# A two-layer trunk with attention and experts: feature-major second attention, a reordered opening, and a router fed by unnormalised rows

## The chip, the cores and the metric

The kernel runs on one core of one Trainium2 chip. The metric is the device time of one execution in microseconds (us), as the median of several runs. The engines are TensorE (PE in the profile), VectorE (DVE), ScalarE (ACT), GpSimd (POOL) and SyncE (SP, which issues most of the transfers).

## What is computed

Two layers over 256 positions of width 1024, one sequence. All of it is float32; the large products are made of three products of a high and a low part (`w_hi`, `w_lo`). For the parts that the change touches the reference says:

```python
mod = (cond @ ada_w[layer] + ada_b[layer])[:, None, :]
sh_m, sc_m, g_m, sh_f, sc_f, g_f = jnp.split(mod, 6, axis=-1)
h = _rmsnorm(x, gn[0]) * (1.0 + sc_m) + sh_m          # ahead of each of the four sub-layers
x = x + g_m * _rmsnorm(y, gn[1])                      # behind it

# second layer's attention (8 heads; 128 plain + 64 rotated features each)
c_q, c_kv, k_rope = jnp.split(h @ w_in, [256, 384], axis=-1)
q = (_rmsnorm(c_q, g_q) @ w_q_up).reshape(B, S, 8, 192)
kv = (_rmsnorm(c_kv, g_kv) @ w_kv_up).reshape(B, S, 8, 256)
# rotate q_rope and k_rope by position, causal softmax of q.k * 192**-0.5, times v, @ w_out

# second layer's experts
logits = (h @ w_router) + b_router                    # top 2 of 8, softmax of the two
```

The first layer has a stick-breaking attention and a dense gated product of width 2816.

## The kernel before

**Stages.** In order of time: the opening (sum of `ada_w` over the 8 parts of the condition vector, first normalisation), the first attention (to about 157 us), the dense product (to 359), the second attention (to 479), the router (to 504), eight or more visits to experts of some 47 us each, and the combination.

**Weights.** SyncE brings pieces of up to 128x2048 (1 MB) into a ring of six in one fixed order, `stream`; it issues piece n when piece n-6 is freed (`freed`). For a weight piece, ScalarE makes the high part (`hi`, L515) once the product before last is done (`used`), VectorE the low part (`lo`, L837), which frees the slot, and TensorE then multiplies. For a piece of `ada_w`, VectorE alone adds it to `acc` scaled by one column of the condition (L850, L853). Each engine has its own handwritten order and the semaphores tie them.

**Modulation.** `mod_columns` (L1380) is 16 products of one column each on TensorE that sum `acc` over the partitions into shift and scale columns; `mod_cols` on VectorE adds the bias. `transpose_xhat` (L1371) turns the normalised rows into feature-major form. `modulated` (L883, L876) applies scale and shift on VectorE, 128x256 at a time, in four blocks of two; ScalarE casts each block (L557), VectorE makes its low part, and the products wait for it (`hTlo`). `keep_clock` (L1413) are filler products. There are three such boundaries with `modulated`: v=0 in the opening, v=1 ahead of the dense product, v=2 ahead of the second attention. v=3 feeds the router and the experts.

**Second attention.** The products with `mla_in` are token-major, 448 columns wide. ScalarE squares and sums the latents, VectorE scales them (`lat`), TensorE turns them (L1551), VectorE applies the gain (`cT`). q and kv are made token-major; ScalarE copies them out (L682, L688), VectorE rotates (L1082 and on), TensorE turns them back (L1579 to L1597), and four large copies follow. Then scores (L1606, L1607), a mask added by VectorE (L1112), two maxima, exponentials on ScalarE from SBUF, division, turning (L1614), a copy back (L1131), products with the values (L1479) and the output product with four weight pieces.

**Router.** `residual`, then ScalarE sums the squares of the new `x`, VectorE normalises into `xhat`, TensorE turns it (L1652), and 16 products with the router's weights give the logits (L1662). VectorE finds the top two and each row's place (L1175 and on); selection products (L1683) gather the first expert's rows.

## Time and profile before

| | |
|---|---|
| median of 3 runs | 901.51 us (900.4 to 906.21) |
| the profiled execution | 900.82 us |
| its span, first to last instruction | 899.3 us |
| mean granted TensorE clock | 0.972 of full speed |
| TensorE matmul busy | 837.3 us (93%) |
| VectorE busy | 705.9 us (78%) |
| ScalarE busy | 524.3 us (58%) |
| chain that ended last | PE 81%, DVE 12%, ACT 2%, DMA 2% |
| from HBM | 257.82 MB |

The busy share of TensorE is high nearly everywhere, and matmuls are pipelined, so it doesn't say whether the engine does useful work at full speed. The stages at the layer boundaries and the second attention have to be read by themselves, in windows and in order of time. The granted clock has two levels, 1.0 (2.4 GHz) and 0.5 (1.2 GHz); a mean between them is a mix in time. A float32 product shows as two records.

### The profile page before, as it was taken

The page shows a single profiled execution, that of the slowest core. Times are in us where ns is not written, and L with a number is a line of the kernel's source. Part 1 is how long each engine was busy: PE and PEld are TensorE (multiplying, and loading weights), DVE is VectorE, ACT ScalarE, POOL GpSimd, SP SyncE. Part 2 cuts the span into 40 slices and gives each one's busy share as a digit, 9 for nine tenths or more (in the row PEclk, how much of TensorE's full clock was granted, in tenths as well). Part 3 has the DMA queues.
Part 4 walks back from the last instruction along what each step waited for, and adds up shares of the span by engine and source line. Part 5 has one row for each costly group of instructions (what it writes and reads, how often), then busy time and mean ns, then how long its engine had stood idle before and what let it go on. Part 6 is the DMA issues. An engine that isn't in the chain of part 4 may idle for free.

```text
span 899.3 us, 12482 instructions
## 1 busy us (share of the span) xinstructions
PE 837.3 (93%) x4720; PEld 741.3 (82%) x4720; DVE 705.9 (78%) x585; ACT 524.3 (58%) x531; POOL 37.9 (4%) x46
## 2 busy tenths in 40 slices
PE   2999999899999999988798899999999999999993
PEld 2999777899999888877677788888888888888882
DVE  4888677876666988553855988898988889898977
ACT  2224924444444434334545678787979787878873
POOL 1001001000000101010000300000000000000120
PEclk9899999899999999689999999999999999999998
DMA  9989867297778998379912799999999999999991
GB/s 341 410 306 377 302 253 286 97 353 262 268 271 300 368 344 322 117 264 420 390 47 61 254 396 343 422 359 419 360 408 360 408 365 406 385 386 393 368 373 47
DMA packets 46239, 283.52 MB, mean 315 GB/s; under 512 B 5855, under 2 KB 5858, under 8 KB 19834
## 3 DMA queue, kind: packets, MB, share of 16 engines
q1 hardware_dynamic: 41002, 268.80, 77.7%
q0 software_dynamic: 3312, 12.06, 3.3%
q10 hardware_dynamic: 1888, 2.15, 0.7%
q8 instruction: 26, 0.43, 0.2%
q14 instruction: 11, 0.09, 0.0%
HBM read 257.82 MB, written 25.17 MB: 315 GB/s over the span
## 4 chain that ended last, share of the span: by engine, by line
PE 81%; DVE 12%; ACT 2%; DMA 2%; issue 2%; ACTq 1%; DVEq 0%; SPq 0%
PE ps L1712 9%; PE ps L1713 9%; PE ps L1717 9%; PE ps L1358 6%; PE ps L1360 6%; PE ps L1361 6%; PE ps L1320 5%; PE ps L1322 5%; PE ps L1321 5%; PE ps L1735 4%; PE ps L1729 4%; PE ps L1730 4%; DVE acc L853 3%; DVE w_lo L837 2%; PE ps L1380 2%; DMA ring<-in_moe_w_down 2%
## 5 line engine op out<-in xcount | busy, mean ns | idle before, releaser
L1169 DVE TENSOR_TENSOR w_lo<-ring,w_hi 128x2048 fp32r<-128x2048 f32 (+1 forms) x96 | 209.7, 2202 | 38.1 <-ACT w_hi L733 36.8
L515 ACT ACTIVATE w_hi<-ring 128x2048 fp32r<-128x2048 f32 (+2 forms) x58 | 109.7, 1893 | 198.0 <-PE ps L1361 100.6
L837 DVE TENSOR_TENSOR w_lo<-ring,w_hi 128x2048 fp32r<-128x2048 f32 (+2 forms) x58 | 138.3, 2385 | 77.1 <-ACT w_hi L515 77.1
L733 ACT ACTIVATE w_hi<-ring 128x2048 fp32r<-128x2048 f32 (+1 forms) x96 | 175.7, 1839 | 20.4 <-PE ps L1717 11.9
L1358 PE MATMUL ps<-hT_lo,w_hi 128*128 128x256 f32 x480 | 137.8, 287 | 4.6 <-DVE hT_lo L876 2.4
L1360 PE MATMUL ps<-hT_hi,w_hi 128*128 128x256 f32 x480 | 136.7, 285 | 0.0
L1361 PE MATMUL ps<-hT_hi,w_lo 128*128 128x256 f32 x480 | 136.7, 285 | 0.0
L853 DVE SCALAR_TENSOR_TENSOR acc<-ring,cond,acc 128x2048 f32<-128x2048 f32 x42 | 98.7, 2349 | 2.7
L1712 PE MATMUL ps<-w_hi,xe_hi 128*128 128x512 f32 (+1 forms) x256 | 97.7, 382 | 2.5 <-DVE xe_lo L1243 2.5
L1358 PEld LDWEIGHTS ps<-hT_lo,w_hi 128*128 128x128 f32 x480 | 93.2, 194 | 5.7 <-issue 2.8
L1169 DVE TENSOR_TENSOR m_lo<-ring,m_hi 128x2048 fp32r<-128x2048 f32 (+2 forms) x48 | 92.7, 1932 | 6.3 <-ACT m_hi L733 6.3
L1713 PE MATMUL ps<-w_hi,xe_lo 128*128 128x512 f32 (+1 forms) x256 | 96.3, 376 | 0.0
L1360 PEld LDWEIGHTS ps<-hT_hi,w_hi 128*128 128x128 f32 x480 | 93.2, 194 | 0.0
L1361 PEld LDWEIGHTS ps<-hT_hi,w_lo 128*128 128x128 f32 x480 | 93.1, 194 | 0.0
L733 ACT ACTIVATE m_hi<-ring 128x2048 fp32r<-128x2048 f32 (+2 forms) x48 | 78.0, 1625 | 8.9 <-PE ps L1717 6.4
L1717 PE MATMUL ps<-w_lo,xe_hi 128*128 128x512 f32 (+1 forms) x256 | 65.1, 376 | 0.0
L1712 PEld LDWEIGHTS ps<-w_hi,xe_hi 128*128 128x128 f32 x256 | 48.1, 188 | 9.9 <-issue 2.6
L1713 PEld LDWEIGHTS ps<-w_hi,xe_lo 128*128 128x128 f32 x256 | 48.1, 188 | 7.3
L1717 PEld LDWEIGHTS ps<-w_lo,xe_hi 128*128 128x128 f32 x256 | 47.4, 188 | 7.7
L1729 PE MATMUL ps<-w_hi,eT_hi 128*128 128x512 f32 x128 | 50.7, 396 | 0.0
L1730 PE MATMUL ps<-w_hi,eT_lo 128*128 128x512 f32 x128 | 50.0, 391 | 0.0
L1320 PE MATMUL ps<-w_lo,hT_hi 128*128 128x512 f32 (+1 forms) x112 | 45.4, 405 | 3.7 <-DVE hT_lo L876 2.1
(289 smaller groups left out, 1442.2 us busy)
## 6 DMA issues: line engine op xcount, KB each, us to landing
ring<-in_moe_w_gu SPq DMA_DIRECT2D x64, 1024.0 KB, 7.1
ring<-in_ada_w SPq DMA_DIRECT2D x48, 1024.0 KB, 6.9
ring<-in_moe_w_down SPq DMA_DIRECT2D x40, 1024.0 KB, 8.3
ring<-in_moe_w_gu SPq DMA_DIRECT2D x32, 768.0 KB, 8.9
ring<-in_ffn_w_gu SPq DMA_DIRECT2D x22, 1024.0 KB, 5.0
ring<-in_sb_w_in SPq DMA_DIRECT2D x12, 1024.0 KB, 7.5
ring<-in_ffn_w_down SPq DMA_DIRECT2D x11, 1024.0 KB, 6.1
x_rows<-blank SPq DMA_DIRECT2D x1, 8704.0 KB, 27.1
```

What stands on the lines that cost most here:

```text
L515: act.activation(w_hi[m % 2][:, 0:cols_n], ring[n % R][:, 0:cols_n], ACT.Copy).then_inc(hi_done, 1)
L733: act.activation(m_hi[k % NB][:, 0:n_c], ring[(N0 + k) % R][:, 0:n_c], ACT.Copy).then_inc(hi_done, 1)
L837: dve.tensor_tensor(w_lo[m % 2][:, 0:cols_n], ring[n % R][:, 0:cols_n], w_hi[m % 2][:, 0:cols_n].bitcast(F32), ALU.subtract).then_inc(free ...
L853: dve.scalar_tensor_tensor(dst, ring[n % R][:, :], cond[:, k:k + 1], dst, ALU.mult, ALU.add).then_inc(freed, 1)
L1169: dve.tensor_tensor(m_lo[k % NB][:, 0:n_c], ring[(N0 + k) % R][:, 0:n_c], m_hi[k % NB][:, 0:n_c].bitcast(F32), ALU.subtract).then_inc(free ...
L1320: pe.matmul(out, a_hi, b_lo, start=start, stop=False)
L1358: pe.matmul(o, w_h, hT_lo[:, k0 + k, :], start=(begin and k == 0 and f % 2 == 0), stop=False, skip_group_check=True)
L1360: pe.matmul(o, w_h, hT_hi[:, k0 + k, :], start=False, stop=False, skip_group_check=True)
L1361: ins = pe.matmul(o, w_l, hT_hi[:, k0 + k, :], start=False, stop=(end and k == 3 and f % 2 == 1), skip_group_check=True)
L1712: pe.matmul(o, xe_hi[:, 2 * q + h, :], bh[:, h, s, :], start=q + h == 0, stop=False)
L1713: pe.matmul(o, xe_lo[:, 2 * q + h, :], bh[:, h, s, :], start=False, stop=False)
L1717: ins = pe.matmul(ps[:, 2 * j + s, 0:gw[j]], xe_hi[:, 2 * q + h, :], bl[:, h, s, :], start=False, stop=q == 3 and h == 1)
```

## The change

1. **Opening.** ScalarE issues only the transfers of `x`, the latent gains, the frequencies and the positions ahead of its first work; those of the router and the gate biases go behind the first normalisation, whose scaling it now does itself. VectorE adds the eighth piece of `ada_w` in two halves, and TensorE sums the shift half while the scale half is added. `hi(1)` goes behind `modulated_hi(0)`.
2. **Modulation.** Of the four blocks, VectorE makes 0 and 3, ScalarE 1 and 2. Of `mod_columns(3)` only the shift half stays ahead of the second attention, the scale half goes to the router stage. Fillers ahead of the second attention are 5+5 instead of 8+8.
3. **Second attention.** All is feature-major: `mla_in` (padded to 512 columns, the rotated key twice) and both up-projections are computed transposed. The q latents aren't normalised; the root of their squares (`qs`, by token) is the scale of the exponential. The kv latents are scaled by a reciprocal of 128x256. Rotation is a product with a sign-and-swap matrix (`turn_half`) and with tables `trigT`. The causal mask is one float32r product per head (`later_r`). Exponentials are read from PSUM. Two of the four copies of turned probabilities go to ScalarE.
4. **Router.** TensorE turns `x` itself; logits are multiplied by the reciprocal root of the row where the bias is added. `xhat` is made by ScalarE behind the first expert piece's `hi`.

The core of the diff (long runs of the old second attention, declarations and host layout are left out):

```diff
 # ScalarE
+            for c in range(TC):
+                act.wait_ge(rstd_done, c + 1)
+                act.activation(xhat[:, c, :], x[:, c, :], ACT.Copy, scale=rstd[:, 0, c:c + 1]).then_inc(xhat_done, 1)
             act.dma_start(wr[:, :, :], w_router[0].rearrange("(k p) n -> p k n", p=P)).then_inc(s_small, 16)
             act.dma_start(br[:, :], b_router).then_inc(s_small, 16)
...
             hi(0)
+            modulated_hi(0)
             hi(1)
-            modulated_hi(0)
...
+                modulate(1)
+                for b in range(4):
+                    if b == 2:
+                        modulate(2)
+                    if b in (0, 3):
+                        act.wait_ge(t_done, 2 * v + b // 3 + 1)
+                    else:
+                        act.wait_ge(t_act, 2 * v + b)
...
             hi(M + 2)
+            act.wait_ge(cT_ok, 1)
+            act.activation(cT_hi[:, 0:2, :], cT[:, 0:2, :], ACT.Copy).then_inc(cThi, 1)
+            act.activation(sq[:, 0:2, :].rearrange("p k t -> p (k t)"), ps[:, 0, :], ACT.Square).then_inc(sq_ok, 1)
+            act.wait_ge(used, M + 2)
+            act.activation(sq[:, 2, :], ps[:, 1, 0:T], ACT.Square).then_inc(sq_ok, 1)
+            act.activation(kra[:, :], ps[:, 1, T:2 * T], ACT.Copy).then_inc(kra_ok, 1)
             hi(M + 3)
...
+            act.wait_ge(sum_mm, 1)
+            act.activation(root_kv[:, :], ps[:, 0, 0:T], ACT.Sqrt, scale=1.0 / KVL, bias=eps[:, 0:1]).then_inc(root_kv_ok, 1)
+            act.activation(qs[:, :], ps[:, 0, T:T + TC], ACT.Sqrt, scale=float(QW) / QL, bias=eps[:, 1:2]).then_inc(qs_ok, 1)
+            act.wait_ge(cT_ok, 2)
+            act.activation(cT_hi[:, 2, :], cT[:, 2, :], ACT.Copy).then_inc(cThi, 1)
             hi(M + 4)
...
             ehi(0, 0)
+            x_turned(1)
+            squares(6, 1, x[:, 1, :], mjunk)
+            root(6, 1)
+            for c in range(TC):
+                act.wait_ge(rstd_done, TC * 6 + c + 1)
+                act.activation(xhat[:, c, :], x[:, c, :], ACT.Copy, scale=rstd[:, 6, c:c + 1]).then_inc(xhat_done, 1)
             ehi(0, 1)
 # VectorE
-            ada(2)
-            normalise(0)
-            ada(DC - 2)
+            ada(3)
+            for c in range(TC):
+                inverse_root(0, c)
+            ada(DC - 4)
...
+            for a, done in ((0, ada_half), (1, freed)):
+                half = slice(a * D, (a + 1) * D)
+                dve.scalar_tensor_tensor(acc[:, half], ring[n % R][:, half], cond[:, n:n + 1], acc[:, half], ALU.mult,
+                                         ALU.add).then_inc(done, 1)
             lo(0)
...
             lo(M + 2)
+            dve.wait_ge(lat_q, 1)
+            for k in range(2):
+                ins = dve.tensor_scalar(cT[:, k, :], ps[:, 0, k * T:(k + 1) * T], lat_g[:, k:k + 1], None, ALU.mult)
             ins.then_inc(cT_ok, 1)
...
             lo(M + 3)
+            dve.wait_ge(kt_ok, 1)
+            dve.wait_ge(root_kv_ok, 1)
+            link(dve.reciprocal(root_kv[:, :], root_kv[:, :]))
+            dve.tensor_tensor(cT[:, 2, :], kt[:, :], root_kv[:, :], ALU.mult).then_inc(cT_ok, 1)
+            dve.wait_ge(qs_ok, 1)
+            dve.reciprocal(qs[:, :], qs[:, :]).then_inc(qs_ok, 1)
+            dve.wait_ge(qra_ok, 1)
+            cos, sin = (trigT[:, n, :].unsqueeze(1).broadcast_to([P, 4, T]) for n in range(2))
+            dve.tensor_tensor(qrT[:, :, :], qra[:, :, :], cos, ALU.mult).then_inc(qr_ok, 1)
+            dve.wait_ge(cThi, 2)
+            dve.tensor_tensor(cT_lo[:, 2, :], cT[:, 2, :], cT_hi[:, 2, :].bitcast(F32), ALU.subtract).then_inc(cTlo, 1)
+            lo(M + 4)
+            dve.wait_ge(kr_mm, 1)
+            dve.wait_ge(cT_ok, 2)
+            link(dve.tensor_tensor(kt[:, :], ps[:, 1, 0:T], trigT[:, 1, :], ALU.mult))
...
+            link(dve.tensor_tensor(qt[:, :, :], ps[:, 2:4, :].rearrange("p b (a t) -> p (b a) t", a=2), sin, ALU.mult))
+            dve.tensor_tensor(qrT[:, :, :], qrT[:, :, :], qt[:, :, :], ALU.add).then_inc(qr_ok, 1)
...
             row_max(0)
+            lo(M + 1)
             row_max(1)
...
+            residual(2, 5, [ps[:, 0:2, :], ps[:, 2:4, :]], 0)
+            mod_scale(3, 7)
...
             x_turned(0)
             x_turned(1)
+            dve.tensor_copy(lg_add[:, :], ps[:, 7, 0:E]).then_inc(bias_ok, 1)
 # TensorE
+            mod_columns(2, 0, (0,))
+            pe.wait_ge(trig_ok, 1)
...
+            mod_columns(2, 0, (1,))
+            keep_clock(5, 2)
+            mod_columns(3, 0, (0,), 2 * DC)
+            keep_clock(5, 2)
             transpose_xhat(2, 4)
+            gate_spread(2, 2)
...
+                product_T(M + h, 4 * h, 0, h == 0, h == 1, v=2, half_way=lat_q if h == 1 else None)
...
+            q_up(0)
+            pe.wait_ge(sq_ok, 2)
+            pe.wait_ge(kt_ok, 1)
...
+            pe.matmul(ps[:, 1, 0:T], turn_half[:, :], kra[:, :], start=True, stop=True).then_inc(kr_mm, 1)
+            q_up(1)
...
+                if h == 0:
+                    pe.wait_ge(kr_ok, 2)
+                if h == 2:
+                    pe.wait_ge(qs_ok, 1)
+                if h == 4:
+                    pe.wait_ge(qr_ok, 2)
...
+            turn_rows(0)
+            mod_columns(3, 7, (1,))
+            keep_clock(2, 6)
+            turn_rows(1)
```

## Rows read from the trace of the kernel before

**Rows 1.** Two windows: start:end, us, busy us (instructions), clock, DMA share, GB/s
```profile
12.00:33.00 21.00, 15.22 (x109) 14.65 (x110) 19.99 (x15) 6.19 (x11) 0.00 (x0) 1.00 1.03 413
358.90:380.10 21.20, 19.13 (x113) 18.89 (x112) 10.52 (x20) 7.14 (x12) 0.00 (x0) 0.68 0.33 124
```

**Rows 2.** Timeline of the opening: start us, us, engine line op, [idle before <-releaser]
```profile
10.63 1.28 ACT L551 ACT_TABLE_LOAD   x1 [10.63 <-issue]
17.98 14.62 DVE L853 SCALAR_TENSOR_TENSOR acc<-ring,cond,acc 128x2048 f32<-128x2048 f32 x6
30.70 1.91 ACT L515 ACTIVATE w_hi<-ring 128x2048 fp32r<-128x2048 f32 x1 [14.36 <-DMA ring<-in_sb_w_in]
32.65 2.29 DVE L837 TENSOR_TENSOR w_lo<-ring,w_hi 128x2048 fp32r<-128x2048 f32 x1
36.86 0.17 DVE L894 TENSOR_TENSOR shift<-ps,cols 128x8 f32<-128x8 f32 x1 [1.92 <-PE ps L1380]
40.26 0.55 PE L1358 MATMUL ps<-hT_lo,w_hi 128*128 128x256 f32 x1
```

**Rows 3.** Timeline of the boundary ahead of the second attention
```profile
358.87 3.63 PE L1380 MATMUL ps<-ones,acc 128*128 128x1 f32 x32
364.90 6.83 PE L1380 MATMUL ps<-ones,acc 128*128 128x1 f32 x32
377.48 1.90 DVE L883 TENSOR_SCALAR t<-ps,scale,shift 128x256 f32<-128x256 f32 x4 [9.82 <-PE ps L1371]
380.12 0.44 PE L1320 MATMUL ps<-w_lo,hT_hi 128*128 128x448 f32 x1 [2.10 <-DVE hT_lo L876]
```

**Rows 4.** Timeline of TensorE in the second attention
```profile
397.81 1.51 PE L1551 MATMUL ps<-ident,lat 128*128 128x128 f32 x6 [4.30 <-DVE kr L1061]
...
402.99 0.69 PE L1320 MATMUL ps<-w_lo,cT_hi 128*128 128x384 f32 x1
...
415.53 0.50 PE L1320 MATMUL ps<-w_lo,cT_hi 128*128 128x512 f32 x1 [1.73 <-ACT qn L682]
...
431.30 0.46 PE L1606 MATMUL ps<-knT,qnT 128*128 128x128 f32 x2 [1.16 <-DVE krT L1103]
...
434.00 0.39 PE L1606 MATMUL ps<-knT,qnT 128*128 128x128 f32 x2
...
455.65 0.50 PE L1320 MATMUL ps<-w_lo,hT_hi 128*128 128x512 f32 x1 [0.48 <-DVE hT_lo L1136]
```

**Rows 5.** Timeline of the router stage, TensorE and VectorE
```profile
478.95 1.88 PE L1390 MATMUL ps<-acc,ones 128*128 128x512 f32 x4
482.21 1.23 DVE L916 TENSOR_TENSOR x<-x,xhat 128x1024 f32<-128x1024 f32 x1
487.62 3.64 PE L1662 MATMUL ps<-wr_mod,xT 128*128 128x8 f32 x32
492.03 0.17 DVE L1175 TENSOR_TENSOR lg<-ps,lg_add 128x16 f32<-128x16 f32 x1
503.94 0.49 PE L1712 MATMUL ps<-w_hi,xe_hi 128*128 128x512 f32 x1 [2.46 <-DVE xe_lo L1243]
```

**Rows 6.** Groups by form, ScalarE: line, op, forms xcount | busy us, mean ns
```profile
L754 ACT ACTIVATE xe<-ps,shift,scale 128x128 f32<-128x128 f32 x4 | 1.5, 456 | 1.3 <-PE ps L1683 1.3
```

**Rows 7.** Timeline of TensorE at the boundary ahead of the dense product
```profile
169.50 0.58 PE L1358 MATMUL ps<-hT_lo,w_hi 128*128 128x256 f32 x1 [0.47 <-DVE hT_lo L876]
```

**Rows 8.** Chain of waits: start us, us, what (a product of 256 columns)
```profile
46.66 0.12 PE ps L1358
```

**Rows 9.** Groups by form, VectorE, 355 to 506 us
```profile
L837 DVE TENSOR_TENSOR w_lo<-ring,w_hi 128x2048 fp32r<-128x2048 f32 x5 | 11.4, 2291 | 20.7 <-ACT w_hi L515 20.7
L858 DVE RECIPROCAL rstd<-rstd 128x1 f32<-128x1 f32 x12 | 2.0, 163 | 11.7 <-ACT rstd L528 11.5
L1065 DVE TENSOR_SCALAR cT<-ps,lat_g 128x256 f32<-128x256 f32 x3 | 1.3, 476 | 1.7 <-PE ps L1551 1.7
L1121 DVE RECIPROCAL rsum<-psum_p 128x4 f32<-128x4 f32 x4 | 0.7, 174 | 0.0
```

562 lines of the change are left out of this document (305 added, 257 removed).

## Prediction

> **What bounds the kernel now.** I read three views in this order: the table of windows, the timelines of TensorE, VectorE and ScalarE where a window shows TensorE waiting or slow, and the groups of instructions by form for the prices. The reader should see this. From 12 to 33 us the DMA engines are full (share 1.03, 413 GB/s), so the opening has two bounds close together, the transfers and VectorE's chain of `ada` sums [rows 1, 2]. At the layer boundaries TensorE runs at half clock (a mean of 0.68 from 358.9 to 380.1, so mostly 1.2 GHz) and is itself what others wait for: VectorE stood idle 9.82 us before its first modulation, for TensorE's transposes [rows 1, 3]. In the second attention, from 397.81 to 455.65, TensorE is handed from one eviction to the next: idle 4.30 us for `kr`, 1.73 for `qn`, and 24 us lie between the first scores and the output product [rows 4]. The expert visits, from 503.94 on, are not touched [rows 5]; what is saved before them is saved at the end, as the whole stretch before is one chain.
>
> **Opening.** ScalarE's first instruction comes at 10.63 because seven transfers are issued ahead of it ("issue") [rows 2]. The change puts the router's and the biases' transfers behind the normalisation; its queue is then free some 6 us earlier and VectorE can begin about 3 us earlier. It also loses two scalings of `x` (they go to ScalarE, which idles there for 14.36 us) [rows 2]. But the `ada` pieces arrive no earlier: the engines are full. A piece is 1.05 MB, at 413 GB/s 2.5 us. The first attention weight is handed to ScalarE at 30.70 [rows 2], so the last `ada` piece before it is there at about 28.2, and its two halves (2.36/2 us each) end at 30.6, where the whole ended at 32.6 [rows 2]. The modulation's columns come after that in half the time, because the shift half is already done: 30.6+0.2+2.1=32.9 against 36.86. The new bound is `lo(0)`: its `hi` ends at 30.70+1.9=32.6 and it takes 2.29, so 34.9 [rows 2]. Modulation starts at about 35.0+0.5 and the products about 2.6 us later, 38.1 against 40.26 [rows 2]. **Gain 2.2 us**; it is nothing if the order of the transfers makes the weights 2 us later, and 3.5 if they come earlier.
>
> **Modulation split between two engines.** ScalarE's scaled copy of 128x128 takes 456 ns, so one of 128x256 about 0.5 by a slope of 0.1 us per 128 (2048 columns take it 1.91); two are 1.0 us, beside VectorE's two of the same length [rows 2, 6]. The first block gets no earlier; the second comes about 1.1 us earlier. At the second boundary TensorE waited for just that block at 169.50 [rows 7]. **Gain 1.0 us**, between 0 and 1.5. The multiplications moved to ScalarE are hidden there; if ScalarE took as long as VectorE plus its own cast in series, the gain is 0.
>
> **Third boundary.** Before: 32 records of columns from 358.87, a filler, 32 more from 364.90 that take 6.83 us at the lower clock where the first took 3.63, a filler; the first transposed block reaches VectorE at 377.48 [rows 3]. After: three halves (3 x 1.8), four 128x128 products for the angle tables (eight records of 0.13, 1.0), fillers of 5+5 instead of 8+8 (2.5): 8.7 us at full clock, so the transposes start at 367.6, about when `xhat` is ready. If the clock falls at the same distance as before (some 5 us in), the rest doubles and they start at 371. Before, the second filler ended at 375.2 (364.90+6.83 and 16 records of 0.22). The gain has the bounds 4 and 8 us. Half-size groups with fillers between are nearer to the full-clock end, but the clock fell once at each boundary: **I take 6 us**.
>
> **Second attention**, counted from X, the moment that was 377.48. Warm 128x256 products are 0.12 us apart [rows 8].
> - Products with `mla_in`: they start at X+2.6, as before (380.12) [rows 3]. Now 96 of 0.12 us instead of 48 of 448 columns: 11.5 us, plus 1.5 for the cold start; ended X+15.7, where the old one ended X+14.2. The gate spread is put in the idle 2.10 us ahead of them.
> - Up-projection of q: was at 402.99, X+25.5 [rows 4], after squares, roots, `lat`, six transposes, `cT` and the cast. Now the q half of the latents is ready at the half-way signal (X+12.8); two scalings of 476 ns, cast 0.6 and difference 0.7 end at X+15.4 [rows 9], so q starts at X+15.7. **Here 10 us go.**
> - q, sums, turns: 36 products (4.3), sums of squares (1.3) and the turn of `kra` (0.45), 36 products (4.3), four turns of 256 columns fp32 (1.75): X+27.8. Before, q took until 415.53 less its wait, 12.5 us; now 12.1.
> - VectorE beside it: `kt` and `kra` 1.3, `lo` 1.8, then reciprocal, product with the root, `qs`, the cosine product (1.23 like the 128x1024 addition [rows 5]), difference 0.4; `lo(kv_up)` ends at X+27.4 (2.29) [rows 9]. Behind it the rotation: k 1.3, q 2.5, ended X+31.3. TensorE needs the first at X+27.8 and the second after four heads, so it waits about 0.9 and 1.3 us. Queued behind these waits are the second half of the keys and the values (12 products of 512 columns, 2.75): done X+35.6.
> - First scores: X+35.6, where they were 431.30, X+53.8 [rows 4]. **18 us gone by here**: kv's copies in eight pieces, 32 transposes back, and two evictions of 2048 columns are no more.
> - Softmax: a pair of heads costs TensorE 2.7 us (431.30 to 434.00) [rows 4] and 0.25 more for the mask product. VectorE loses the mask addition, but gets `lo` between the first two maxima. Two of four turned copies go to ScalarE. By my walk through the three queues the output product starts at X+56.2, 20.6 us after the first scores; before it was 455.65, X+78.2, 24.4 after them [rows 4].
>
> **Gain 22 us.** All unknown steps are small ones on VectorE. The reciprocal of 128x256 has no row; four columns take 174 ns, one takes 163, so by their slope (3.7 ns a column) 256 take 1.1 us [rows 9]; as other operations of that width it is 0.45. I take 0.45, as most of VectorE's forms cost the same at one width, and keep 1.1 for the range: everything behind it moves with it. Four columns are too few for the trace to refuse it.
> The 64-partition halves of the rotated key are priced like full ones of 256 columns. If each of the some twelve handovers costs 0.3 us more than I gave, the gain is 18; if DVE's rotation does not finish ahead of TensorE at all and the table load of Exp comes late, 14. If there are no waits, 25.
>
> **Router.** Before: the products end at 478.95, the second half of `x` is complete at 483.4, logits 487.62 plus 3.64, VectorE's routing from 492.03, first expert product at 503.94 [rows 5]. Now the transposes take `x` itself: the turned copies end at 485.7, after scale columns, `wr_mod` and a first half of logits; logits end 488.5, routing starts 488.7, 3.4 us earlier. The cut of the first expert piece is no longer ahead of it (it fits beside the logits). But `xhat` now has ScalarE's two scalings (2 us) ahead of `ehi(0,1)`; after two table loads `ehi(0,2)` ends at 497.4 and its `lo` at 499.7, from which the inputs are 1.3+0.7 us away: first product at 501.7. One microsecond is lost so. **Gain 2.3 us**, between -1 and 4.
>
> **Sum**: 2.2+1.0+6+22+2.3=33.5 us. The profiled execution took 900.8 us with what lies around its span of 899.3; 900.8-33.5=867.3. The median of the runs shown is 0.7 above it: **868 us**.
>
> **Rivals.**
> - *A: as above*, 868 (862 to 873): 0.62.
> - *B: VectorE becomes the bound of the second attention.* For it: between X+16 and X+34 it has hardly 2 us of idle time in my plan, and every handover goes over it. Against: in the old stage it waited as TensorE did, and much of that work is gone. Gain there 14 instead of 22: 876. Chance 0.18. The upper price of the reciprocal by itself gives 869, within A. (By the repeat count in the Trainium skill, "VectorE: DVE Perf Modes", walkthrough, it would be 870; I give this 0.4.)
> - *C: the clock.* If the boundary stays at 1.2 GHz as before and the products of `mla_in` and q run at it too (24 us nominal, a quarter of it cold beyond what I gave costs 6, and 2 more go at the boundary): 876. For: the small column products are the same. Against: there are no longer 4 to 6 us of idleness behind them. Chance 0.07.
> - *D: more overlap*, full clock at the boundary and no waits in attention: 868-2-3-1=862 or less. Chance 0.09.
> - *E: slower than before.* TensorE stays at 1.2 GHz from 359 to the router. Nearly all of the stretch is TensorE work (about 75 us nominal), doubled it costs 75 and eats the 33. It decides from about 34 us of nominal work run cold; the time would be 900 to 940. In the old trace the window with the most column products still had a mean clock of 0.68, with more idle time [rows 1]. Chance 0.02.
> - *F: does nothing.* The gained time is taken back by late expert weights (the blank rows of `x_rows` and `y_rows` go out ahead of them). That would give 890 to 901; the router stage comes some 30 us earlier but the transfers move earlier too, by over 5. Chance 0.02.
>
> **Numbers.** Faster by over 1% is under 892.5 us: A to D, 0.96. Within 1%: 0.02; slower: 0.02 (1% is about what a measurement of this kernel can tell from no change). The range holds A and D and reaches to B and C: 861 to 878.
>
> **What would show it.** Opening: ScalarE's first table load before 5 us, first product at about 38.1. Third boundary: columns to transposes under 9 us; idle of VectorE there under 4. Attention: q starts within 1 us of the end of `mla_in`; first scores 33 us behind the first product, output product 54 behind it; the reciprocal's duration. Router: 22 to 23 us from the end of the output product to the first expert product. It is wrong if VectorE waits little and TensorE much between `mla_in` and the first scores (B), or if cold stretches are longer than in the old trace (C).

## The result and the profile after

The changed kernel takes 872.95 us (median of four runs, 868.24 to 875.37), the kernel before 903.1 us beside it (900.4 to 906.21). The ratio is 0.9664, with a 95% interval of 0.9624 to 0.9703. The profiled execution took 873.32 us, its span is 871.8 us; before they were 900.82 and 899.3. So the change gave 30 us by the medians and 27.5 us from profile to profile; the forecast was a sum of 33.5 us and 868 us, range 861 to 878.

The two spans, cut at the same events on TensorE, show where the 27.5 us are. X is the start of the third boundary's modulation.

| stretch | before, us | after, us | gain | forecast |
|---|---|---|---|---|
| start to first product | 40.26 | 40.11 | 0.15 | 2.2 |
| to the columns of the second boundary | 116.94 | 116.05 | 0.9 | |
| to the first gate product | 10.88 | 12.57 | -1.7 | 1.0 |
| to the end of the down product | 190.79 | 190.74 | 0.05 | |
| to X | 18.61 | 14.41 | 4.2 | 6 |
| X to the output product | 78.17 | 55.36 | 22.8 | 22 |
| output product | 23.30 | 23.22 | 0.1 | |
| to the first expert product | 24.99 | 22.56 | 2.4 | 2.3 |
| to the end | 395.36 | 396.78 | -1.4 | |

**The opening.** Timeline of the changed kernel, ScalarE, TensorE and VectorE: start us, us, engine line op, [idle before <-releaser].

```profile
12.82 0.47 ACT L534 ACTIVATE rstd<-ssq,eps 128x1 f32<-128x1 f32 x2
17.32 0.22 DVE L915 RECIPROCAL rstd<-rstd 128x1 f32<-128x1 f32 x2
17.52 1.15 ACT L599 ACTIVATE xhat<-x,rstd 128x1024 f32<-128x1024 f32 x1 [4.23 <-DVE rstd L915]
18.72 3.67 PE L1458 MATMUL ps<-ident,xhat 128*128 128x128 f32 x16 [10.16 <-ACT xhat L599]
22.18 10.47 PE L1501 MATMUL ps<-ones 128*128 128x128 f32 x90
27.68 2.48 DVE L1014 SCALAR_TENSOR_TENSOR acc<-ring,cond,acc 128x1024 f32<-128x1024 f32 x2 [0.23 <-DMA ring<-in_ada_w]
32.19 2.29 DVE L894 TENSOR_TENSOR w_lo<-ring,w_hi 128x2048 fp32r<-128x2048 f32 x1 [2.03 <-ACT w_hi L521]
32.49 1.84 PE L1467 MATMUL ps<-ones,acc 128*128 128x1 f32 x16
34.95 2.11 PE L1467 MATMUL ps<-ones,acc 128*128 128x1 f32 x16
37.09 0.17 DVE L951 TENSOR_TENSOR shift<-ps,cols 128x8 f32<-128x8 f32 x1 [2.61 <-PE ps L1467]
40.11 0.36 PE L1443 MATMUL ps<-hT_lo,w_hi 128*128 128x256 f32 x1
```

VectorE and the transfers did what was forecast: both halves of the last piece end at 30.2 and `lo(0)` at 34.5. But VectorE then waits 2.61 us for the columns (1.92 in [rows 2]). These stand on TensorE behind 90 filler products (45 fp32 products, two records each) that run in one piece from 22.18 to 32.65, although the shift half of the last piece is added by 29.0. The fillers start so late because `x` is scaled only after the reciprocals at 17.32. ScalarE had the roots for them ready at 13.3, 3 us earlier than before (16.3), but in VectorE's new order three `ada` pieces stand ahead of the reciprocals, and ScalarE waits 4.23 us. Before the change the transposes came 1.5 us earlier:

```profile
17.26 3.68 PE L1371 MATMUL ps<-ident,xhat 128*128 128x128 f32 x16 [8.77 <-DVE xhat L870]
```

**Third boundary and second attention.**

```profile
363.85 2.31 PE L1501 MATMUL ps<-ones 128*128 128x128 f32 x10
365.95 3.41 PE L1467 MATMUL ps<-ones,acc 128*128 128x1 f32 x16
369.22 2.48 PE L1501 MATMUL ps<-ones 128*128 128x128 f32 x10
373.88 0.99 DVE L938 TENSOR_SCALAR t<-ps,scale,shift 128x256 f32<-128x256 f32 x2 [3.83 <-PE ps L1458]
376.71 0.36 PE L1443 MATMUL ps<-hT_lo,w_hi 128*128 128x256 f32 x1 [0.21 <-DVE hT_lo L931]
388.36 0.36 PE L1653 MATMUL ps<-cT_hi,w_hi 128*128 128x256 f32 x1
394.67 1.75 DVE L1148 RECIPROCAL root_kv<-root_kv 128x256 f32<-128x256 f32 x1 [2.35 <-ACT root_kv L712]
399.17 2.29 DVE L894 TENSOR_TENSOR w_lo<-ring,w_hi 128x2048 fp32r<-128x2048 f32 x1 [0.76 <-ACT w_hi L521]
401.83 0.85 DVE L1164 TENSOR_TENSOR krT<-krT,kt 64x256 f32<-64x256 f32 x2
402.83 0.36 PE L1653 MATMUL ps<-cT_hi,w_hi 128*128 128x256 f32 x1 [2.40 <-DVE krT L1164]
405.25 0.38 PE L1653 MATMUL ps<-cT_hi,w_hi 128*128 128x256 f32 x1 [0.80 <-DVE qrT L1169]
409.47 0.38 PE L1717 MATMUL ps<-knT,qnT 128*128 128x128 f32 x2
```

X is 373.88. The up-projection of q begins at X+14.5, the first scores at X+35.6, the output product at X+55.4; in [rows 4] these stand at X+25.5, X+53.8 and X+78.2. The reader should see three things: a half of the columns that takes 3.41 us at the lower clock (1.84 at the higher), the reciprocal of 1.75 us, and TensorE's waits of 2.40 and 0.80 us for VectorE.

**The granted clock.** Windows of the changed kernel: start:end, us, busy us (instructions) of PE, PEld, DVE, ACT, POOL, granted clock, DMA share, GB/s. The first answers to the second of [rows 1].

```profile
355.00:376.00 21.00, 21.00 (x117) 19.37 (x115) 13.22 (x19) 12.21 (x21) 2.40 (x1) 0.76 0.46 168
393.00:400.00 7.00, 7.00 (x55) 6.76 (x54) 4.54 (x6) 3.71 (x7) 0.00 (x0) 1.00 1.03 422
452.00:475.00 23.00, 19.08 (x128) 17.11 (x126) 20.80 (x51) 18.68 (x27) 6.31 (x4) 0.85 0.35 108
```

Summed over windows of 1 us (a window with 0.50 counts as 1 us, others in proportion), TensorE was at 1.2 GHz for 44.4 us between 30 and 480 us before the change and for 30.7 after it. Most of these stretches begin among or within a microsecond behind one-column products, fillers, transposes and 8-column products; those of the old second attention, at 397.6 and 442.0, begin while TensorE waits (4.30 and 3.27 us, ahead of transposes), and one at 380.5 just behind such a wait. What lies behind 480 us is not in the sum: every profile has another 5 to 12 us at the lower clock there, all in its last 13 us.

### The profile page after: what moved, and what is told of

Read it like the earlier page. It is cut to its first block, busy times and chain, and to the rows that moved or that the text cites. A ratio compares the mean times of both kernels' runs of the same rounds, so it can differ in the third digit from the quotient of the medians.

```text
span 871.8 us, 12499 instructions
## 1 busy us (share of the span) xinstructions
PE 825.6 (95%) x4732; PEld 731.1 (84%) x4732; DVE 694.8 (80%) x553; ACT 532.0 (61%) x540; POOL 35.5 (4%) x47
## 4 chain that ended last, share of the span: by engine, by line
PE 84%; DVE 9%; DMA 3%; ACT 2%; issue 1%; SPq 0%; DVEq 0%; ACTq 0%
PE ps L1843 9%; PE ps L1844 9%; PE ps L1848 9%; PE ps L1443 6%; PE ps L1446 6%; PE ps L1445 6%; PE ps L1405 4%; PE ps L1407 4%; PE ps L1406 4%; PE ps L1866 4%; PE ps L1860 4%; PE ps L1861 4%; PE ps L1501 3%; DVE w_lo L894 2%; PE ps L1467 2%; DMA ring<-in_moe_w_down 2%
## 5 line engine op out<-in xcount | busy, mean ns | idle before, releaser
L1250 DVE TENSOR_TENSOR w_lo<-ring,w_hi 128x2048 fp32r<-128x2048 f32 (+1 forms) x96 | 209.9, 2202 | 36.7 <-ACT w_hi L784 34.9
L521 ACT ACTIVATE w_hi<-ring 128x2048 fp32r<-128x2048 f32 (+1 forms) x58 | 110.2, 1900 | 168.3 <-PE ps L1446 102.8
L894 DVE TENSOR_TENSOR w_lo<-ring,w_hi 128x2048 fp32r<-128x2048 f32 (+1 forms) x58 | 138.6, 2390 | 63.6 <-ACT w_hi L521 63.5
L784 ACT ACTIVATE w_hi<-ring 128x2048 fp32r<-128x2048 f32 (+1 forms) x96 | 176.0, 1840 | 20.3 <-PE ps L1848 13.1
L1443 PE MATMUL ps<-hT_lo,w_hi 128*128 128x256 f32 x512 | 146.2, 286 | 4.6 <-DVE w_lo L894 2.4
L1446 PE MATMUL ps<-hT_hi,w_lo 128*128 128x256 f32 x512 | 145.6, 284 | 0.0
L1445 PE MATMUL ps<-hT_hi,w_hi 128*128 128x256 f32 x512 | 145.5, 284 | 0.0
L1443 PEld LDWEIGHTS ps<-hT_lo,w_hi 128*128 128x128 f32 x512 | 98.9, 193 | 6.2 <-issue 3.9
L910 DVE SCALAR_TENSOR_TENSOR acc<-ring,cond,acc 128x2048 f32<-128x2048 f32 x41 | 96.3, 2350 | 4.4 <-DMA ring<-in_ada_w 2.2
L1445 PEld LDWEIGHTS ps<-hT_hi,w_hi 128*128 128x128 f32 x512 | 99.0, 193 | 0.0
L1446 PEld LDWEIGHTS ps<-hT_hi,w_lo 128*128 128x128 f32 x512 | 98.9, 193 | 0.0
L1843 PE MATMUL ps<-m_hi,xe_hi 128*128 128x384 f32 (+1 forms) x128 | 46.9, 367 | 0.0
```

The source lines that it names most:

```text
L521: act.activation(w_hi[m % 2][:, 0:cols_n], ring[n % R][:, 0:cols_n], ACT.Copy).then_inc(hi_done, 1)
L784: act.activation(m_hi[k % NB][:, 0:n_c], ring[(N0 + k) % R][:, 0:n_c], ACT.Copy).then_inc(hi_done, 1)
L894: dve.tensor_tensor(w_lo[m % 2][:, 0:cols_n], ring[n % R][:, 0:cols_n], w_hi[m % 2][:, 0:cols_n].bitcast(F32), ALU.subtract).then_inc(free ...
L910: dve.scalar_tensor_tensor(dst, ring[n % R][:, :], cond[:, k:k + 1], dst, ALU.mult, ALU.add).then_inc(freed, 1)
L1250: dve.tensor_tensor(m_lo[k % NB][:, 0:n_c], ring[(N0 + k) % R][:, 0:n_c], m_hi[k % NB][:, 0:n_c].bitcast(F32), ALU.subtract).then_inc(free ...
L1443: pe.matmul(o, w_h, hT_lo[:, k0 + k, :], start=(begin and k == 0 and f % 2 == 0), stop=False, skip_group_check=True)
```

## The experiments

One table serves all of them. Each kernel's profile is cut at the same events as above; "expert visit" is the distance between the first products of two visits (from the second visit on they agree within 0.06 us in each profile), "low clock" the sum just defined. The time is that of the profiled execution, and for e9_all and e10_all_nofill the median of four runs. Every other variant ran once, so its total may not be set against that of the changed kernel (868.24 to 875.37 in four runs): the distances between events in one trace carry the argument. In e4_rot, e9_all and e10_all_nofill a stretch of 3.4 us at the lower clock falls into the first expert visit, which takes 1.6 to 1.7 us more there.

```
kernel          first    2nd bound.  down end  q up to  out end to  expert  low    time
                product  to gate     to mla_in scores   expert      visit   clock
before          40.26    10.88       21.25     28.31    24.99       47.45   44.4   900.8
changed         40.11    12.57       17.24     21.11    22.56       47.72   30.7   873.3
e1_fill         37.65    12.56       17.19     21.13    22.6        47.72   30.7   872.4
e2_root         38.23    10.92       17.30     23.84    22.5        47.73   34.1   872.5
e3_norecip      40.37     9.43       17.22     19.58    23.6        47.73   27.3   869.6
e4_rot          40.49     9.42       17.32     18.40    22.3        47.73   27.3   867.8
e5_nofill3      40.62    10.91       12.57     21.53    26.8        47.73   34.2   871.2
e6_fill2        40.43     9.73       17.31     20.99    22.4        47.72   27.3   870.8
e7_nosplit      40.55    12.64       17.32     21.97    26.8        47.70   44.4   881.8
e8_pad          40.50     9.41       12.40     21.92    26.8        47.45   27.3   866.3
e9_all          37.48     9.43       17.09     18.51    22.3        47.45   27.3   864.7
e10_all_nofill  37.35    12.56       12.63     18.51    23.9        47.45   34.1   863.3
e11_padbase     40.42    10.90       12.40     21.99    26.8        47.73   27.3   870.7
e12_third       40.30    10.90       12.40     22.05    26.8        47.45   27.3   868.4
```

### Opening: fewer fillers (e1_fill), earlier reciprocals (e2_root)

```diff
             for k in range(3, DC):
                 pe.wait_ge(freed, k)
-                keep_clock(9)
+                keep_clock(5)
```

> The changed kernel with five instead of nine filler products behind each ada piece in the opening (50 records instead of 90). Theory 1 (the fillers are the bound of the opening): in the changed kernel TensorE's transposes begin only at 18.7 us, the 90 filler records then run without a gap from 22.2 to 32.6 and the columns of the shift half, ready at 30.2, wait for them. With 50 records they end by 30.2, the columns start at once, the scale columns end 2.0 us earlier and VectorE is bound by lo(0), ended at 34.5: modulation from about 35.0, first product at 38.0 instead of 40.1, and the whole kernel about 2 us shorter, which only the profile can tell. Theory 2 (the fillers hold TensorE's clock): with gaps between them the columns run at 1.2 GHz, 3.5 us a half instead of 1.8, and the first product is not earlier than 40.1. Theory 3 (the weights are the bound): lo(0) ends later than 35 and nothing moves.

```diff
-            ada(3)
+            ada(2)
             for c in range(TC):
                 inverse_root(0, c)
-            ada(DC - 4)
+            ada(DC - 3)
```

> The changed kernel with VectorE's two reciprocals of the opening behind two ada pieces instead of three, the fillers as they were. They then stand at 14.8 us instead of 17.3, ScalarE scales x 2.5 us earlier, the transposes begin at about 16.2 instead of 18.7. Theory 1 (the fillers are the bound because they start late): the same 90 records then end at about 30.5 (the last nine wait for the piece before last, ended 27.5), the columns start 2 us earlier and the first product comes at about 38.0. Theory 2 (clock or weights): first product within 0.3 us of 40.1, as in the changed kernel.

Timeline of TensorE and VectorE with five fillers:

```profile
22.45 6.86 PE L1501 MATMUL ps<-ones 128*128 128x128 f32 x50
29.27 1.95 PE L1467 MATMUL ps<-ones,acc 128*128 128x1 f32 x16
31.83 1.84 PE L1467 MATMUL ps<-ones,acc 128*128 128x1 f32 x16
34.65 0.16 DVE L951 TENSOR_TENSOR shift<-ps,cols 128x8 f32<-128x8 f32 x1
37.65 0.36 PE L1443 MATMUL ps<-hT_lo,w_hi 128*128 128x256 f32 x1 [2.08 <-DVE hT_lo L931]
```

The columns no longer make VectorE wait: its `shift` at 34.65 follows `lo(0)` at once, and the first product comes 2.46 us earlier. The columns ran at the higher clock. With the reciprocals earlier the transposes start at 16.35 and the first product comes at 38.23:

```profile
16.35 3.68 PE L1458 MATMUL ps<-ident,xhat 128*128 128x128 f32 x16 [7.29 <-ACT xhat L599]
```

Both ways remove the same delay, so it is shown: the change moved `x`'s scaling, and with it the fillers, onto the path. Of the 2.46 us the span shows only 1.0 (870.8 against 871.8): 1.0 goes before the second boundary (117.09 us from the first product to its columns instead of 116.05) and 0.4 behind the first expert product.

### The reciprocal (e3_norecip) and VectorE's order (e4_rot)

```diff
-            link(dve.reciprocal(root_kv[:, :], root_kv[:, :]))
+            link(dve.tensor_scalar(root_kv[:, :], root_kv[:, :], 0.5, None, ALU.mult))
```

> The changed kernel with the reciprocal of the 128x256 root left out (a multiplication by 0.5 of the same width stands in its place, so the values are not those of the reference). Its record in the changed kernel is 1.75 us; the multiplication takes 0.42. Theory V (VectorE sets the pace from the sums of squares to the scores): cT, its cast, lo(kv_up) and both rotations all move by 1.3 us, TensorE's wait for krT (2.40 us) shrinks by as much, and the first scores come 1.3 us earlier after the end of the mla_in products (20.0 us instead of 21.3). Theory T (TensorE or ScalarE's cast of kv_up sets it): 0.3 us or less.

The values are then not those of the reference; the run serves for its times alone.

```profile
390.79 0.30 DVE L1148 TENSOR_SCALAR root_kv<-root_kv 128x256 f32<-128x256 f32 x1 [2.20 <-ACT root_kv L712]
```

The multiplication took 0.30 us. From the start of the q up-projection to the first scores there were 19.58 us instead of 21.11: 1.53 us against a difference of 1.45 in the record. So what VectorE saves at this place reaches the scores in full.

```diff
+            hi(M + 4)
             act.wait_ge(cT_ok, 2)
             act.activation(cT_hi[:, 2, :], cT[:, 2, :], ACT.Copy).then_inc(cThi, 1)
-            hi(M + 4)
...
-            link(dve.tensor_tensor(kt[:, :], ps[:, 1, 0:T], trigT[:, 1, :], ALU.mult))
-            dve.wait_ge(kr_ok, 1)
+            dve.tensor_tensor(kt[:, :], ps[:, 1, 0:T], trigT[:, 1, :], ALU.mult).then_inc(kr_ok, 1)
+            dve.wait_ge(qr_mm, 1)
+            dve.tensor_tensor(qt[:, :, :], ps[:, 2:4, :].rearrange("p b (a t) -> p (b a) t", a=2), sin, ALU.mult)\
+                .then_inc(qr_ok, 1)
+            dve.wait_ge(kr_ok, 2)
             for n in range(2):
                 half = slice(ROPE * n, ROPE * (n + 1))
                 ins = dve.tensor_tensor(krT[half, n, :], krT[half, n, :], kt[half, :], ALU.add)
             ins.then_inc(kr_ok, 1)
-            dve.wait_ge(qr_mm, 1)
-            dve.wait_ge(qr_ok, 1)
-            link(dve.tensor_tensor(qt[:, :, :], ps[:, 2:4, :].rearrange("p b (a t) -> p (b a) t", a=2), sin, ALU.mult))
+            dve.wait_ge(qr_ok, 2)
             dve.tensor_tensor(qrT[:, :, :], qrT[:, :, :], qt[:, :, :], ALU.add).then_inc(qr_ok, 1)
...
             pe.wait_ge(kT_a, 2)
+            pe.wait_ge(kr_ok, 3)
+            pe.wait_ge(qr_ok, 3)
             scores(0)
```

> The changed kernel with two reorderings between mla_in and the scores. ScalarE casts kv_up before it waits for cT (it stood idle 2.19 us there), and VectorE does both sine products of the rotations first and both additions behind them, so that TensorE's key products wait only until the PSUM banks have been read; the scores wait for the additions. Theory V (VectorE's order is the bound): lo(kv_up) ends 0.8 us earlier, the keys wait for one operation of 0.42 instead of three, the fifth head waits for none, and the first scores come 2.5 us earlier (18.8 us after the end of mla_in instead of 21.3). Theory T (TensorE itself is the bound there): its work between is the same and the scores move by less than 0.5. Rival Q (the queue behind): the additions, lo(mla_out) and the value copies then reach VectorE's queue so late that the first row maximum is not earlier than 38.6 us after the start of the second block's modulation, and the output product gains under 1 us.

```profile
394.73 2.28 DVE L894 TENSOR_TENSOR w_lo<-ring,w_hi 128x2048 fp32r<-128x2048 f32 x1
396.93 0.41 DVE L1160 TENSOR_TENSOR kt<-ps,trigT 128x256 f32<-128x256 f32 x1
397.27 1.21 DVE L1162 TENSOR_TENSOR qt<-ps,trigT 128x1024 f32<-128x1024 f32 x1
397.49 0.36 PE L1654 MATMUL ps<-cT_hi,w_hi 128*128 128x256 f32 x1 [0.66 <-DVE kt L1160]
403.16 0.38 PE L1718 MATMUL ps<-knT,qnT 128*128 128x128 f32 x2
```

VectorE's subtraction follows without the wait of 0.76 us, TensorE's wait falls from 2.40 to 0.66, the one of 0.80 is gone, and the scores come 18.40 us behind q instead of 21.11: 2.7 us. The run has two reorderings at once (ScalarE's earlier cast and VectorE's order), and how the 2.7 us divide between them is not shown. Rival Q fell: from the first scores to the end of the output product it is 43.0 us in both. The row maximum starts 3.05 us behind the first scores in both.

### Fillers at the boundaries (e5_nofill3, e6_fill2)

```diff
             mod_columns(2, 0, (1,))
-            keep_clock(5, 2)
             mod_columns(3, 0, (0,), 2 * DC)
-            keep_clock(5, 2)
             transpose_xhat(2, 4)
```

> The changed kernel without the two groups of filler products at the third boundary (20 records, 2.3 and 2.5 us in the changed kernel). Theory F (the fillers are no cover but part of the path): the last columns end about 2.3 us earlier and the transposes follow them as soon as xhat is there (VectorE finishes its second half 8.6 us behind the end of the down product); the transposes end 11.2 us behind the down product instead of 14.4, a gain of 3.2. Theory C (they hold the clock): with the gap before the second half of xhat the clock stays low longer, the mla_in products begin at 1.2 GHz, and of the 3.2 us less than 1 is left at the start of the q up-projection.

```diff
             mod_columns(1, 0)
-            keep_clock(8, 1)
+            keep_clock(2, 1)
             transpose_xhat(1, 4)
```

> The changed kernel with two instead of eight filler products at the second boundary (4 records instead of 16). There the columns end at 3.8 us behind their start, and xhat's second half is ready 6.3 us behind it. Theory F: in the runs in which the clock is low there (fillers of 3.8 us, first gate product 12.6 us behind the first columns), the transposes start 1.3 us earlier and the first gate product comes 1 to 2 us earlier; in a run at full clock (9.4 us) nothing changes, as VectorE is the bound. Theory C: the idle time lowers the clock and the distance is 12.6 us or more.

Timeline of TensorE at the third boundary without fillers:

```profile
359.34 4.78 PE L1467 MATMUL ps<-ones,acc 128*128 128x1 f32 x32
363.98 3.65 PE L1458 MATMUL ps<-ident,xhat 128*128 128x128 f32 x16
```

The stretch from the down product to the `mla_in` products is 4.7 us shorter (12.57 against 17.24). That is no proof that the fillers cost 4.7 us: with all fillers but at full clock the same stretch takes 12.40 (e8_pad, below):

```profile
363.87 1.91 PE L1459 MATMUL ps<-ident,xhat 128*128 128x128 f32 x16
```

These transposes start 8.48 us behind the down product; in the changed kernel, with 10.2 us of the stretch at the lower clock, they start 12.0 behind it. Without fillers 6.8 us of the stretch were at the lower clock, and it was only 0.2 us longer than e8_pad's. So VectorE is the bound without fillers, and the low clock costs little there; with them they lie on the path as soon as the clock is low. At the start of the q up-projection 4.4 of the 4.7 us are left, so theory C, which left less than 1, fell. And the whole kernel is only 2 us faster, as the router stage then took 26.8 us, with 8-column products at the lower clock. Its logits, and below them those of the changed kernel, as long as in [rows 5]:

```profile
452.56 6.83 PE L1790 MATMUL ps<-wr_mod,xT 128*128 128x8 f32 x32
```
```profile
458.25 3.64 PE L1792 MATMUL ps<-wr_mod,xT 128*128 128x8 f32 x32
```

At the second boundary the comparison has to be made between profiles with the same low-clock stretches there (3.4 us from 158 or 159 and 3.4 us from 165 or 166): 9.73 us with two fillers, 10.92 with eight (e2_root). Theory F holds, by 1.2 us (one profile with two fillers; with eight, e5_nofill3, e11_padbase and e12_third give 10.9 as well).

### The split modulation undone (e7_nosplit)

```diff
-                for b in (0, 3):
+                for b in range(4):
                     dve.wait_ge(tr_done, 4 * v + b + 1)
```

(ScalarE's two scaled copies of `modulated_hi` are gone, and VectorE makes each low part behind the next block's modulation.)

> The changed kernel with the modulation of all four blocks on VectorE again, as before the change; everything else stays. Forecast: 1.0 us per boundary where TensorE waits for the second block (it did at the second boundary before the change, 0.5 us in the row), so 0.5 to 1.5 us between the first and the last product of the first weight at each of the three boundaries. Rival (the copies were hidden): the start of the first product behind the last transpose is the same, the second blocks are waited for nowhere, and the distances from the first product of each boundary to the next anchor stay within 0.2 us.

TensorE waited for the second block again in the opening and at the third boundary:

```profile
41.96 0.39 PE L1427 MATMUL ps<-hT_lo,w_hi 128*128 128x256 f32 x1 [0.34 <-DVE hT_lo L917]
379.92 0.39 PE L1427 MATMUL ps<-hT_lo,w_hi 128*128 128x256 f32 x1 [0.46 <-DVE hT_lo L917]
```

The `mla_in` products took 12.36 us to the q up-projection instead of 11.65, while the first of them came 0.2 us sooner behind X (2.64 against 2.83). So the split is worth about 0.5 us at this boundary and 0.3 in the opening, at most half of the forecast. At the second boundary, whose wait of 0.47 us the forecast started from, TensorE waited for no second block in this run either; there the two stretches, to the first gate product and from it to the end of the down product, are 0.1 and 0.3 us longer, with low-clock stretches of the same length. The kernel as a whole took 8.5 us more, which this does not explain: it had 13.7 us more at the lower clock, which cost 6.9 us if TensorE set the pace all the while. Half of the 8.5 us lie in the router (26.8 instead of 22.6). 1.6 us are left for three boundaries, within what was expected, but they are the rest of an estimate.

### Where the expert visits lost 1.8 us (e8_pad, e11_padbase, e12_third)

The visits' code is the same in both kernels, yet a visit takes 47.72 us after the change and 47.45 before it. The change made the tiles ahead of the accumulator 64 bytes smaller in each partition.

```diff
+        sb("pad", [P, 16])
         acc_at = cursor[0]
         acc = sb("acc", [P, 6 * D])
```

> The changed kernel with 64 bytes of unused SBUF ahead of the large accumulator, so that this and all tiles behind it (the expert visit's inputs and its third weight buffer among them) lie again where they lay before the change; no instruction differs. In five profiles of the changed kernel and of variants of it one expert visit takes 47.72 us, in the profile of the kernel before 47.45, with the same instructions and no waits in between: 1.9 us over seven visits. Theory P (the place in SBUF): the period goes back to 47.45. Theory N (it is not the place): it stays at 47.72.

```diff
         acc = sb("acc", [P, 6 * D])
+        sb("pad", [P, 16])
```

> The changed kernel with the 64 bytes behind the accumulator instead of ahead of it: the third weight buffer, the selections and the accumulator stay where the changed kernel has them, the expert's inputs (xe, eT) and all other tiles behind it lie where they lay before. If it is the place of the inputs that TensorE loads as weights or of the tiles beside them, the visit takes 47.45 us as with the padding ahead; if it is the third weight buffer or the accumulator, it stays at 47.72.

```diff
         acc = sb("acc", [P, 6 * D])
+        sb("pad", [P, 16])
...
-        m_hi = w_hi + [sb("m_hi2", [P, PIECE], F32R, at=acc_at + 8192)]
-        m_lo = w_lo + [sb("m_lo2", [P, PIECE], F32R, at=acc_at + 16384)]
+        m_hi = w_hi + [sb("m_hi2", [P, PIECE], F32R, at=acc_at + 8192 + 64)]
+        m_lo = w_lo + [sb("m_lo2", [P, PIECE], F32R, at=acc_at + 16384 + 64)]
```

> The kernel with the 64 bytes behind the accumulator, and beside it the third weight buffer (its high and its low part) moved up by 64 bytes, so that it lies where it lay before the change; only the accumulator and the small tiles laid over it (selection, squares) stay where the changed kernel has them. If the third weight buffer's place sets the period of a visit, it takes 47.45 us; if it is the accumulator's or the selection's place, 47.72.

The first product of the second and of the third visit: the changed kernel (47.70 us apart), then with the padding ahead of the accumulator (47.45 apart):

```profile
522.79 0.40 PE L1843 MATMUL ps<-w_hi,xe_hi 128*128 128x512 f32 x1
570.49 0.40 PE L1843 MATMUL ps<-w_hi,xe_hi 128*128 128x512 f32 x1
```
```profile
518.77 0.39 PE L1844 MATMUL ps<-w_hi,xe_hi 128*128 128x512 f32 x1
566.22 0.39 PE L1844 MATMUL ps<-w_hi,xe_hi 128*128 128x512 f32 x1
```

The same two products with the third weight buffer back in place as well (e12_third, 47.46 apart; with the padding behind the accumulator alone, e11_padbase, 47.73):

```profile
519.35 0.39 PE L1844 MATMUL ps<-w_hi,xe_hi 128*128 128x512 f32 x1
566.81 0.39 PE L1844 MATMUL ps<-w_hi,xe_hi 128*128 128x512 f32 x1
```

With the accumulator and all tiles behind it back in place the visit takes 47.45 us, with only the tiles behind the accumulator in place 47.73, with the third weight buffer in place as well 47.45. So it is the place of the third weight buffer. The visits explain only 1.8 of the 7 us by which e8_pad's profile is shorter than the changed kernel's; most of the rest is the clock, which was high at the second and the third boundary and low in the router. The dense product has an effect of its own: among the profiles without low clock in it, it takes 188.82 us with 64 bytes anywhere (e8_pad, e9_all, e11_padbase, e12_third) and 189.25 without (e3_norecip, e4_rot, e5_nofill3); its cause is open. Why a buffer 64 bytes lower slows the 512-column products that read the other two buffers as well is open. The groups by form, changed kernel and padded kernel (busy us, mean ns):

```profile
L1843 PE MATMUL ps<-w_hi,xe_hi 128*128 128x512 f32 x192 | 76.1, 397 | 2.1 <-DVE xe_lo L1328 2.1
```
```profile
L1844 PE MATMUL ps<-w_hi,xe_hi 128*128 128x512 f32 x192 | 75.6, 394 | 2.1 <-DVE xe_lo L1329 2.1
```

### Together (e9_all, e10_all_nofill)

> The changed kernel with what the runs before showed, together: 64 unused bytes ahead of the accumulator (a visit of 47.45 us instead of 47.72, 1.9 us in all), five fillers instead of nine behind each ada piece (first product 2.4 us earlier), kv_up cast ahead of the wait and both sine products ahead of the additions (first scores 2.7 us earlier behind mla_in). If the parts add up: 872.9 - 7.0 = 866. Rival K (the clock takes it back): the low-clock stretches between 30 and 480 us, 30.7 us in the changed kernel's profile and 27 to 34 in most of the others, differ from run to run by the moments at which the stages come; with 44 us of them the time is about 5 us above the sum, 871, and with 27 it is 2 below, 864.

> The same as the kernel beside it, and without the two filler groups at the third boundary. There the profile gave a distance from the down product to the first mla_in product of 12.6 us without fillers, 17.2 with fillers at low clock and 12.4 with fillers at full clock. Theory F (fillers on the path): 2 to 4 us less than the kernel beside it. Theory K (the clock decides, not the fillers): within 1 us of it, either way, and the difference follows the low-clock stretches.

The first took 864.69 us (four runs, 863.57 to 865.7), ratio to the kernel before 0.9613, interval 0.9547 to 0.9678; the second 863.29 us (861.86 to 864.8), ratio 0.9591, interval 0.9527 to 0.9656. Against the changed kernel (ratio 0.9664, measured apart from them) they are 8 and 10 us below its median, where the parts add up to 7 for the first. But the two kernels and the changed one did not run beside each other, and as shares of the kernel before the difference is 0.5 and 0.7%, with intervals that overlap. Between the two, the third boundary gained 4.5 us, and 3.1 went at the second boundary, 1.5 up to the down product and 1.6 in the router, with 34.1 us of low clock instead of 27.3: mostly theory K. Both are faster than the kernel before. That they are faster than the changed kernel is likely, as all eight times lie below its four (865.7 and less against 868.24 and more), but not settled; nor is which of the two is better (1.4 us apart, intervals overlap).

## Why the prediction was right, step by step

**The forecast as a whole** held: 872.95 lies 5 us above the likeliest value and inside its case A (862 to 873) to the edge. What differs is where the us came from: the profile shows 27.5 us of gain where the sum had 33.5, and part of the 27.5 is the clock, which the sum did not count on (below). That the time fell into the range is thus partly luck. Of the signs named, ScalarE's first table load (3.50), VectorE's idle time at the third boundary (3.83), the first scores (32.8 us behind the first product) and the router (22.6) came as written; the first product (40.11, not 38.1), the distance from columns to transposes (12.0, not under 9) and the reciprocal did not.

**Opening, 2.2 forecast, 0.15 measured.** The terms for VectorE, the transfers and `lo(0)` were right within 0.5 us. The step that failed is "the modulation's columns come after that in half the time": it priced the columns, and not what stands ahead of them in TensorE's queue. The fillers there are 10.5 us long and begin when the transposes end, and the transposes began 1.5 us later than before, because the three microseconds that ScalarE gained were lost again by VectorE's order. e1_fill and e2_root gave 2.5 and 1.9 us.

**Split modulation, 1.0 forecast.** The wait of [rows 7] is gone as foretold, but the stretch to the first gate product became 1.7 us longer, as its fillers and transposes fell into the lower clock (12.6 us; 9.4 at full clock in four of the profiles). The edit itself is worth 0.3 to 0.5 us at each boundary (e7_nosplit), at most half of the forecast.

**Third boundary, 6 forecast, 4.2 measured.** The two ends were right: 8.7 us (its terms add up to 8.9) from the down product to the transposes at full clock (8.48 in e8_pad, e11_padbase and e12_third), start at about 371 if the clock falls (371.50 measured). I took a value between the two, where a run shows one or the other.

**Second attention, 22 forecast, 22.8 measured; first scores at X+35.6 as forecast.** This is where the change's gain is. It is read from the timelines; no run takes a part of the new attention back, so how the gain divides between its parts is argued and not shown. Two errors cancelled. q began 1.2 us earlier than I had it (X+14.5), as no cold start came at `mla_in`. And VectorE, rival B, was indeed the bound between the sums of squares and the scores: TensorE waited 3.2 us for it instead of the 2.2 forecast, mainly because the reciprocal takes 1.75 us and not 0.45. e3_norecip and e4_rot show that 1.5 and 2.7 us more were to be had there. The gain also has a part of the clock in it: before, the stretches from 380.5, 397.6 and 442.0 us ran at 1.2 GHz for 3.4, 10.2 and 3.4 us; after, only the first 0.4 us behind X did. If TensorE set the pace in all of them, that is 8.3 of the 22.8 us, so at the same clock the gain lies between 14.5 and 22.8. The prediction's comparison of the two up-projections of q has a slip: it calls 12.5 us the old one "less its wait", but 415.53 less 402.99 is 12.5 with the wait of 1.73 in it, and 10.8 without; the new stretch of 12.1 was no gain over that. The sum, which goes by the time from X, does not use it.

The reciprocal's price by a slope over four columns was 1.1 us: (1.75-0.17)/252 columns is 6.3 ns a column, not 3.7. The Trainium skill ("VectorE: DVE Perf Modes", "Walkthrough: the 8-slice pipeline in each mode", "First, the fixed hardware budget") calls it an iterative divide with a repeat count of 8, from which I had estimated 2.3 us; the trace lies nearer to that than to the price that I took.

**Router, 2.3 forecast, 2.4 measured.** Right in this profile, although 6.8 us of it ran at the lower clock. No run shows the new stage without low clock, and the old one (24.99 us) had none in it, so at the same clock the gain would be larger than 2.4; that the number fits is partly luck. The spread was missing: 26.8 us instead of 22.5 in five of the other profiles, which is more than the whole gain of this part.

**Behind the router, nothing forecast, -1.4 measured.** From the first expert product to the first of the last visit it was 334.07 us instead of 332.27, by a buffer's place in SBUF (332.26 in e8_pad); what is behind it gave 0.4 back.

**Rivals.** C (the clock) went the other way for this profile: 13.7 us less at the lower clock, worth up to 6.9 of the 27.5 us. The kernel before has it too: of seven runs of it on one chip one took 2922.21 us and is left out, and six took 893.8, 894.9 and 895.5 us at a mean granted clock of 0.977 to 0.979, and 900.7, 903.2 and 903.4 at 0.968 to 0.970. The changed kernel's four runs took 868.2 to 875.4 at 0.975 to 0.983. Compared at the same mean clock (0.977: 894.9 and 872.6; 0.979: 893.8 and 895.5, and 873.3), though perhaps on different chips, the gain is 21 to 22 us, where 33.5 were forecast. That figure is worked out and was not measured by an experiment. The four runs of the kernel before that stood beside the changed one (900.4 to 906.21) were all of the longer kind, so the 30 us by the medians are the upper end.

## What to carry to other kernels

An engine's queue has to be priced with everything in it, work that only keeps the clock included: moved by an edit, it lands on the path. Where the next engine only waits for a buffer to be read, signal after the read and put the rest of the computation behind it; together with an earlier cast on ScalarE that gave 2.7 us here for no work. And when a profile loses time where nothing was edited, compare where its buffers lie and the granted clock of its stretches before looking for a wait.

## What the hardware showed that I had not expected

- 64 bytes of difference in the place of one weight buffer made an expert visit 0.27 us longer (47.70 to 47.75 in nine profiles, 47.45 in the five with the buffer in its old place), 1.8 us up to the last visit.
- A reciprocal of 128x256 takes 1.75 us on VectorE, one of 128x2 0.16, one of 128x4 0.17; a multiplication of 128x256 took 0.30 to 0.48.
- The same stage, with the same instructions, takes 22.3 to 26.8 us (router) and 12.4 or 17.2 us (third boundary), and this goes with the granted clock: with 6.8, 10.2 and 17.1 us of the router stage at 1.2 GHz it took 22.3 to 22.6, 23.6 to 23.9 and 26.8 us; the third boundary with its fillers took 12.4 with none and 17.1 to 17.3 with 10.2. The profiles are of kernels that differ elsewhere, one each; whether the edit or the single run decides where the low stretches fall is not shown. Their sum between 30 and 480 us was 27.3 to 44.4 us over fourteen profiles.
